# An expert stage in which the 16 prompt rows lie as 128 rows of 128 columns

## What is computed

```python
cap = CAPACITY_FACTOR * T // N_EXPERTS          # 16 prompt rows, 256 sample rows
aff = softmax(h @ w_router)
gates, idx = top_k(aff.T, cap)
xg = h[idx]
y = (silu(xg @ w_gate[e]) * (xg @ w_up[e])) @ w_down[e]
y = y * gates
out = zeros.at[idx].add(y)                      # x = x + gate2 * out, then the final RMSNorm
```

## Time and profile before

| | |
|---|---|
| median of 3 runs | 3281.63 us (3280.39 to 3283.32) |
| the profiled execution | 3282.97 us |
| its span in the trace | 3281.2 us |
| PE busy in the span | 3083.0 us (94%) |
| expert stage | about 1961 us to the end |

### The profile page before, as it was taken

One profiled execution on the slowest core, in us unless ns is written; L12 is line 12 of the kernel. 1 busy time (PEld: TensorE's weight loads), 2 busy tenths in 40 slices (PEclk: granted clock), 3 DMA queues, 4 the chain that ended last, 5 costly groups with the idle time before them and its releaser, 6 DMA issues. The chain is left out here.

```text
span 3281.2 us, 58620 instructions
## 1 busy us (share of the span) xinstructions
PE 3083.0 (94%) x21488; PEld 2804.2 (85%) x21488; DVE 1850.1 (56%) x3184; ACT 1710.9 (52%) x3368; POOL 422.2 (13%) x396
## 2 busy tenths in 40 slices
PE   8999997899999999999899749999999999999996
PEld 4788886688888888888788649999999999999995
DVE  3222225788888888888533485445455455455455
ACT  3222224577777777777433345454454454544454
POOL 0333335500000000000000010111111111111103
PEclk9999998899999999999899759999999999999998
DMA  6222116400000000000164305566665666666656
GB/s 238 70 74 73 65 57 201 163 17 23 23 19 29 19 22 22 21 27 28 63 205 153 116 31 190 182 190 184 184 190 181 190 186 185 187 189 185 190 171 264
DMA packets 318188, 394.61 MB, mean 120 GB/s; under 512 B 30132, under 2 KB 274312, under 8 KB 317080
## 3 DMA queue, kind: packets, MB, share of 16 engines
q1 hardware_dynamic: 307160, 356.11, 32.8%
q0 software_dynamic: 10560, 36.77, 5.0%
q10 hardware_dynamic: 384, 0.62, 0.1%
HBM read 319.54 MB, written 74.06 MB: 120 GB/s over the span
## 5 line engine op out<-in xcount | busy, mean ns | idle before, releaser
L2654 DVE TENSOR_TENSOR e_w_lo<-e_raw,e_w_hi 128x2048 fp32r<-128x2048 f32 x192 | 440.0, 2292 | 476.2 <-ACT e_w_hi L2584 468.8
L92 PE MATMUL e_ps<-e_x_hi,e_w_hi 128*128 128x272 f32 x2048 | 602.2, 294 | 3.4 <-issue 3.4
L94 PE MATMUL e_ps<-e_x_hi,e_w_lo 128*128 128x272 f32 x2048 | 593.9, 290 | 0.0
L93 PE MATMUL e_ps<-e_x_lo,e_w_hi 128*128 128x272 f32 x2048 | 590.1, 288 | 0.0
L1613 DVE TENSOR_TENSOR a_pT_lo<-a_ps_t,a_pT_hi 128x512 fp32r<-128x512 f32 (+1 forms) x648 | 368.0, 600 | 139.5 <-ACT a_pT_hi L1522 139.1
L1522 ACT ACTIVATE a_pT_hi<-a_ps_t 128x512 fp32r<-128x512 f32 (+1 forms) x648 | 319.4, 532 | 172.4 <-PE a_ps_t L1391 165.3
L92 PEld LDWEIGHTS e_ps<-e_x_hi,e_w_hi 128*128 128x128 f32 x2048 | 386.3, 189 | 5.0 <-issue 3.5
L93 PEld LDWEIGHTS e_ps<-e_x_lo,e_w_hi 128*128 128x128 f32 x2048 | 387.0, 189 | 0.0
L94 PEld LDWEIGHTS e_ps<-e_x_hi,e_w_lo 128*128 128x128 f32 x2048 | 386.0, 188 | 0.0
L2584 ACT ACTIVATE e_w_hi<-e_raw 128x2048 fp32r<-128x2048 f32 x189 | 360.4, 1907 | 0.0
L1586 DVE TENSOR_REDUCE a_mx<-a_ps_s 128x1 f32<-128x896 f32 (+2 forms) x392 | 345.9, 890 | 22.8 <-PE a_ps_s L1381 22.8
(11 more groups left out here) (318 smaller groups left out, 5355.8 us busy)
## 6 DMA issues: line engine op xcount, KB each, us to landing
e_raw<-in_w_gate SPq DMA_DIRECT2D x64, 1024.0 KB, 5.0
e_raw<-in_w_up SPq DMA_DIRECT2D x64, 1024.0 KB, 5.0
e_raw<-in_w_down SPq DMA_DIRECT2D x64, 1024.0 KB, 5.0
s_ret<-p_pr SPq DMA_DIRECT2D x17, 768.0 KB, 3.6
p_raw<-in_w_in SPq DMA_DIRECT2D x8, 1152.0 KB, 18.7
o_cT<-s_ct SPq DMA_DIRECT2D x17, 512.0 KB, 5.0
s_x<-o_x SPq DMA_DIRECT2D x17, 512.0 KB, 5.0
s_xn<-o_xn SPq DMA_DIRECT2D x17, 512.0 KB, 3.4
```

Of the source, the lines that this page charges most:

```text
L92: nc.tensor.matmul(out, w_hi, x_hi, start=first, stop=False)
L93: nc.tensor.matmul(out, w_hi, x_lo, start=False, stop=False)
L94: return nc.tensor.matmul(out, w_lo, x_hi, start=False, stop=last)
L2654: nc.vector.tensor_tensor(w_lo[n % RING][:, :, :], raw[n % RING][:, :, :], w_hi[n % RING][:, :, :].bitcast(F32), ALU.subtract).then_inc(w_ ...
```

## The change

The 16 prompt rows of 1024 columns are handled as 128 rows of 128 columns: partition c * 16 + t holds block c of row t.

- Lists. `hot_c` becomes 128 x 128: it compares slot with `again_b`, which counts 0 to 15 eight times. So each of the 128 partitions gets the number of its row; `token[:, e, 2]` is eight times the row plus `which`, the number of the block. ACT's two copies per expert in `keep` become one. A 0/1 matrix `alike` marks the partitions that belong to one row.
- Rows in. The third gather reads 128 pieces of 512 B into `e_xg_c`. One transpose turns all of it (j = 0); the sample rows are turned four pieces in a row, two blocks at a time (j = 1 to 4): 17 transposes in place of 24, in bursts of 5, 4, 4 and 4 after chunks 3, 4, 5 and 7. DVE gives the prompt part scale and shift in two instructions for all blocks (`context`, in n = 4); ACT keeps the 256-column ones. PE's j = 2 waits for `xc_scaled`, the first of DVE's two.
- Sums out. `e_yT_c` and `e_yg_c` are apart. q = 0 is one transpose for the prompt rows, q = 1 to 4 four each: 17 in place of 24, in bursts of 5, 8 and 4 after chunks 0, 1 and 2. POOL adds the prompt pieces first.
- The end. The sum of squares of a prompt row lies in 8 partitions and is put together by one matmul with `alike`. The weight vector is loaded again as `f_w_c` by eight small transfers on SP. The prompt list goes first through the last norms and scatters.

The core of the diff:

```diff
@@ selection, ACT and DVE
             def keep(e):
                 act.wait_ge(hot_mm, e + 1)
-                nc.scalar.activation(got[:, e, 0:2, :].rearrange("p b v -> p (b v)"), ps_got[e % 2][:, 0:2 * NVAL], ACT.Copy)\
+                nc.scalar.activation(got[:, e, :, :].rearrange("p b v -> p (b v)"), ps_got[e % 2][:, 0:3 * NVAL], ACT.Copy)\
                     .then_inc(got_ok, 1)
-                nc.scalar.activation(got[0:CAP_CTX, e, 2, :], ps_got[e % 2][0:CAP_CTX, AT_C:AT_C + NVAL], ACT.Copy).then_inc(got_ok, 1)
...
+                if r == 1:
+                    nc.vector.tensor_scalar(g["weights"].alike[:, :], dist[:, :], 0.0, None, ALU.is_equal)
+                    nc.vector.tensor_scalar(which[:, :], row16[:, :], 1.0 / CAP_CTX, None, ALU.mult)
...
-                nc.vector.tensor_scalar(hot_c[j][:, :], iota_b[:, 0:CAP_CTX], slot[:, NT, e:e + 1], None, ALU.is_equal)
+                nc.vector.tensor_scalar(hot_c[j][:, :], again_b[:, :], slot[:, NT, e:e + 1], None, ALU.is_equal)
...
-            link(nc.vector.tensor_copy(g["token"][:, :, :].rearrange("p e h -> p h e"), rest[:, 0:3, :]))
+            nc.vector.tensor_copy(g["token"][:, :, 0:2].rearrange("p e h -> p h e"), rest[:, 0:2, :])
+            link(nc.vector.tensor_scalar(g["token"][:, :, 2], rest[:, 2, :], float(DC), which[:, 0:1], ALU.mult, ALU.add))
@@ FirstWeights
-    def gather(self, pool, xn_rows, token):
-        for n, m in enumerate([P, P, CAP_CTX]):
-            pool.indirect_dma_start(self.xg[0:m, n, :], None, xn_rows,
-                                    bass.IndirectOffsetOnAxis(ap=token[0:m, 0, n:n + 1], axis=0)).then_inc(self.xg_in, 16)
+    def fetch(self, pool, rows, token, e):
+
+        for n in range(2):
+            pool.indirect_dma_start(self.xg[:, n, :], None, rows.rearrange("t p d -> (t p) d"),
+                                    bass.IndirectOffsetOnAxis(ap=token[:, e, n:n + 1], axis=0)).then_inc(self.xg_in, 16)
+        pool.indirect_dma_start(self.xg_c[:, :], None, rows.rearrange("t p (c d) -> (t p c) d", d=P),
+                                bass.IndirectOffsetOnAxis(ap=token[:, e, 2:3], axis=0)).then_inc(self.xg_in, 16)
@@ experts
-        SUMS_AFTER = {0: (0, 1), 1: (2, 3), 2: (4, 5)}
-        ROWS_AFTER = {3: (0, 1), 4: (2, 3), 5: (4, 5), 7: (6, 7)}
+        SUMS_AFTER = {0: (0, 1), 1: (2, 3), 2: (4,)}
+        ROWS_AFTER = {3: (0, 1), 4: (2,), 5: (3,), 7: (4,)}
@@ SP
             sp.dma_start(wf[:, :], a["norm_f_w"].rearrange("(o d) -> o d", o=1).broadcast_to([P, D])).then_inc(wf_in, 16)
+            for c in range(DC):
+                sp.dma_start(wf_c[c * CAP_CTX:(c + 1) * CAP_CTX, :],
+                             a["norm_f_w"][c * P:(c + 1) * P].rearrange("(o d) -> o d", o=1).broadcast_to([CAP_CTX, P])).then_inc(wf_in, 16)
@@ PE, turn_rows
-                for n, m in enumerate(ROWS):
-                    ins = nc.tensor.transpose(ps_t[b][:, n * P:n * P + m], xg[0:m, n, c * P:(c + 1) * P],
-                                              g["ident"][0:m, 0:m])
+                elif j == 2:
+                    pe.wait_ge(xc_scaled, e + 1)
...
+                if j == 0:
+                    ins = nc.tensor.transpose(ps_t[b][:, 0:P], xg_c[:, :], g["ident"][:, :])
+                else:
+                    for h in range(2):
+                        for n in range(2):
+                            c = 2 * (j - 1) + h
+                            ins = nc.tensor.transpose(ps_t[b][:, h * CAP + n * P:h * CAP + (n + 1) * P],
+                                                      xg[:, n, c * P:(c + 1) * P], g["ident"][:, :])
                 ins.then_inc(x_turned, 1)
@@ PE, turn_sums
-                for c in range(4):
-                    ins = nc.tensor.transpose(ps_t[q % 2][0:m, c * P:(c + 1) * P], yT[:, half_at * 4 + c, n * P:n * P + m],
-                                              g["ident"][:, :])
+                if q == 0:
+                    ins = nc.tensor.transpose(ps_t[0][:, 0:P], yT_c[:, :, :].rearrange("p c t -> p (c t)"), g["ident"][:, :])
+                else:
+                    n, half_at = (q - 1) // 2, (q - 1) % 2
+                    for c in range(4):
+                        ins = nc.tensor.transpose(ps_t[q % 2][:, c * P:(c + 1) * P], yT[:, half_at * 4 + c, n * P:(n + 1) * P],
+                                                  g["ident"][:, :])
@@ PE, the end
-            for q in range(6):
+            for q in range(SUMS):
                 turn_sums(NE - 1, q)
+                if q == 3:
+                    pe.wait_ge(sq_ok, NTA + 1)
+                    nc.tensor.matmul(ps[0][:, 0:1], early.alike[:, :], ss[:, NTA:NTA + 1], start=True, stop=True).then_inc(ss_c_ok, 1)
@@ ACT, start of expert 0
-            for c in range(0, DC, 2):
-                rows(0, c)
-            act.wait_ge(xT_ok, 2 * DC)
+            rows(0, 1)
+            rows(0, 3)
+            act.wait_ge(xc_ok, 1)
+            act.wait_ge(xT_ok, 2)
+            act.wait_ge(xT_odd, 2)
             nc.scalar.activation(x_hi[:, 0:DC // 2, :], xT[:, 0:DC // 2, :], ACT.Copy).then_inc(x_hi_half, 1)
+            act.wait_ge(xT_ok, DC)
@@ DVE
+            def context(e):
+                dve.wait_ge(x_turned, e * TURNS + 1)
...
+                nc.vector.tensor_tensor(xT[:, :, CAP:SLOTS], ps_t[0][:, 0:P].rearrange("p (c t) -> p c t", c=DC),
+                                        g["gain"][:, 1, :, CTX:CTX + 1].broadcast_to(by_chunk), ALU.mult).then_inc(xc_scaled, 1)
+                dve.wait_ge(xc_scaled, e + 1)
+                nc.vector.tensor_tensor(xT[:, :, CAP:SLOTS], xT[:, :, CAP:SLOTS],
+                                        g["mod"][:, SHIFT2:SHIFT2 + DC, CTX:CTX + 1].broadcast_to(by_chunk), ALU.add).then_inc(xc_ok, 1)
```

More of the change, by code:

```diff
@@ L2011, in selection @@
         iota_i, iota_b = k.sb("s_iota_i", [P, P], I32), k.sb("s_iota_b", [P, P], BF16)
+        again_i, again_b = k.sb("s_again_i", [P, DC, CAP_CTX], I32), k.sb("s_again_b", [P, P], BF16)
+        which = k.sb("s_which", [P, 1])
         row_i = k.sb("s_row_i", [P, 1], I32)
@@ L2017, in selection @@
         hot = [k.sb(f"s_hot{i}", [P, NT, P], BF16) for i in range(2)]
-        hot_c = [k.sb(f"s_hot_c{i}", [P, CAP_CTX], BF16) for i in range(2)]
+        hot_c = [k.sb(f"s_hot_c{i}", [P, P], BF16) for i in range(2)]
         far = k.sb("s_far", [P, ON_ACT, P], BF16)
@@ L2070, in _ @@
             pool.wait_ge(token_ok, 1)
-            g["weights"].gather(pool, s["xn"].rearrange("t p d -> (t p) d"), g["token"])
+            g["weights"].fetch(pool, s["xn"], g["token"], 0)
         @block.tensor
@@ L2347, in experts @@
         AHEAD = 3
-        ROWS = [P, P, CAP_CTX]
-        raw, w_hi, w_lo, xg, weights = early.raw, early.w_hi, early.w_lo, early.xg, early.chunk
+        TURNS, SUMS = 5, 5
+        raw, w_hi, w_lo, xg, xg_c, weights = early.raw, early.w_hi, early.w_lo, early.xg, early.xg_c, early.chunk
         xT = k.sb("e_xT", [P, DC, SLOTS])
@@ L2467, in _ @@
                 scatter(e)
[L2469 removed]
+            pool.wait_ge(x_turned, NE * TURNS)
             pool.wait_ge(y_out, LAST * 48)
[L2471 to L2473 removed]
+            early.fetch(pool, s["x1"], g["token"], LAST)
             pool.wait_ge(half_ok, 1)
@@ L2584, in split, with rows @@
                 nc.scalar.activation(w_hi[n % RING][:, :, :], raw[n % RING][:, :, :], ACT.Copy).then_inc(w_hi_ok, 1)
-            def rows(e, c):
-                if c == 0 and not (isinstance(e, int) and e == 0):
+            def rows(e, j):
+                if j == 1 and not (isinstance(e, int) and e == 0):
                     act.wait_ge(x_lo_ok, e)
-                act.wait_ge(x_turned, e * DC + c + 1)
-                for lo, hi, who in ((0, CAP, LAT), (CAP, SLOTS, CTX)):
-                    nc.scalar.activation(xT[:, c, lo:hi], ps_t[c % 2][:, lo:hi], ACT.Identity,
-                                         bias=g["mod"][:, SHIFT2 + c, who:who + 1],
-                                         scale=g["gain"][:, 1, c, who:who + 1]).then_inc(xT_ok, 1)
+                act.wait_ge(x_turned, e * TURNS + j + 1)
+                for h in range(2):
+                    c = 2 * (j - 1) + h
+                    nc.scalar.activation(xT[:, c, 0:CAP], ps_t[j % 2][:, h * CAP:(h + 1) * CAP], ACT.Identity,
+                                         bias=g["mod"][:, SHIFT2 + c, LAT:LAT + 1],
+                                         scale=g["gain"][:, 1, c, LAT:LAT + 1]).then_inc(xT_ok, 1)
             def rows_hi(e):
-                act.wait_ge(xT_ok, (e + 1) * 2 * DC)
+                act.wait_ge(xT_ok, (e + 1) * DC)
+                act.wait_ge(xc_ok, e + 1)
                 if not (isinstance(e, int) and e == 0):
@@ L2611, in body @@
                     if not last:
-                        for c in ROWS_AFTER.get(n - 1, ()):
-                            rows(e + 1, c)
+                        for j in ROWS_AFTER.get(n - 1, ()):
+                            if j:
+                                rows(e + 1, j)
                         if n == 8:
```

(23 more changed lines are left out.)

173 lines of the change are left out of this document (84 added, 89 removed).

## The result

| us | before | after |
|---|---|---|
| median (4 runs each) | 3281.01 (3280.00 to 3283.32) | 3222.32 (3221.62 to 3224.40) |
| profiled execution | 3282.97, span 3281.2 | 3224.40, span 3222.7 |

The ratio is 0.982, with a 95% interval of 0.9808 to 0.9832: 1.8% faster. The direction and the large term were right, the size was not.

What follows compares the result with a forecast made beforehand. PE was taken to bound the expert loop. Loop -46.8, selection +1.5, start of expert 0 -2.5 and end -1.5 summed to -49.3 us, median 3281.63 to 3232.3, forecast 3232, range 3224 to 3245.

Steps and rivals of the forecast that it cites:

- the large term: Expert loop: fewer, all full transposes on PE save 3.12 us in each of 15 experts, 46.8 us.
- rival 2: PE's transposes: only their count matters, the gap stays in each burst; gain 21 us, 3258; chance 0.05.
- (a): Loop, chunk 4: PE's j = 2 waits for DVE's first prompt instruction, with 0.7 us of slack.
- (b): Loop, chunk 8: PE needs the last `e_h_lo`; with a shorter burst ahead, 0.5 us of slack is left.
- rival 1: Loop: a new wait at (a) or (b) gives back 4.5 to 15 us, 3237 to 3247; chance 0.10.
- The start: Expert 0: fewer turns, half of `e_x_hi` made meanwhile; PE begins at about 1971.8, -2.5 us (0 to -4).
- rival 3: SP's queue blocks on the eight broadcast loads, 15.73 us each: slower, 3346; chance 0.02.
- the end: After the last expert: smaller prompt sums and norms, sample list issued last at about 3269; -1.5 us (+1 to -3).
- the "linear" bound: Loop: a burst's price goes with its length, 34 x 0.109 = 3.71 us an expert, gain 50 us.
- the selection: Routing on DVE: wider one-hot +1.0 us, with other new instructions together +1.5 us.
- the other new instructions: Selection on DVE: `alike` and `which` 0.23 and some 0.15, the split token instruction 0.1 us.
- rival 4: Change does more than said: no price of a burst, start gains 4; 3221; chance 0.08.

Runs made afterwards that it cites:

- b_rows128: Kernel before, prompt list gathered and turned as 128 rows instead of 16, the count of transposes kept: 3255.17 us, ratio 0.9917 to before.
- a_late3: Changed kernel with three unused 128x512 VectorE adds ahead of the prompt instructions in each expert: 3240.63 us.
- a_head_old: Changed kernel, first half of x's high part waiting for all turned rows in expert 0: 11.79 us from stage start to first product, against 10.65.
- a_fw_early: Changed kernel with SP issuing the final norm's weights in expert 0 instead of ahead of the last expert's rows: 3224.91 us.
- b_hotc_wide: Kernel before, VectorE writing the selection's prompt one-hot 128 columns wide while PE reads 16: one-hot loop 2.41 us an expert, as before.
- a_prompt_last: Changed kernel with the prompt list issued last at the end: 1363.1 us from the selection on, against 1362.9.
- b_prompt_first: Kernel before with the last expert's prompt list issued ahead of the two sample lists: 1420.7 us from the selection on, against 1420.2.
- b_sems3: Kernel before with three more, unused semaphores: 8.8 us from last data to end of span, 10.3 from last issue, as before.

## Why the prediction was wrong

**Right, and shown.** PE alone bounds the loop, and every microsecond taken from it counts: period 76.35, PE busy in all of it. The 16-row piece is what costs: b_rows128 gets 1.79 of the 3.33 us by adding rows. The waits on "issue" are gone, and rival 2 (count only) with them. The covers (a) and (b) hold, with 0.7 and 0.3 us that can be used, so rival 1 did not come about; a_late3 shows what it would have cost. The start gave 2.36 of 2.5, by the step named (a_head_old). SP's eight issues cost 0.48 us each, not 15.73, and are hidden (a_fw_early): rival 3 falls.

In the loop, then, the mechanism was right and one price in it was off. At the end 3.3 us came from something that the forecast had no term for.

**Wrong: the price of a full piece.** I split the 0.87 us of a burst of 8 into 8 x 0.099 and 0.08 for the burst. That split rested on one length of burst with full pieces alone, and all the bursts of the earlier trace rows fit it. It is 0.109 a piece and nothing for the burst, the "linear" bound of the text, which stood there at 50 us: 49.8 measured, and the bursts of 4, 5 and 8 leave zero for a burst. The term of 46.8 was 3.0 too small.

**Wrong: the selection.** +1.5 forecast, -0.4 measured. Most of it is the one-hot: I priced the widened one at the pace of its neighbours (0.19) and left the neighbours as they were. It came to 0.16, and the others got faster, which one trace can't tell. A loss was the only sign that I had considered. Off by 1.9, of which b_hotc_wide explains 16 x 0.06 = 1.0. The forecast's 0.5 for the other new instructions was not tested, and the stretch differs by up to 0.6 between traces of kernels that are alike in it.

**Wrong: the end.** -1.5 forecast, bound -3, -4.7 measured. Up to the last issue it is -2.2, in line with the step (the last issue some 2 us sooner); a_prompt_last gives 1.5 of it to the order. I had added that the last sample list would land later after its issue, which it does, by 0.7 to 0.8. But 3.3 us vanished behind the last data. For that stretch I had no term, and no reason for leaving it out; no row showed one, and b_prompt_first, a_prompt_last and b_sems3 did not find one: the cause of the largest part of the miss stays open. Off by 3.2.

**The range.** 3.0 + 1.9 + 3.2, less 0.1 at the start, plus 1.2 us by which this execution reached the selection sooner, is the whole miss of 9.2 between the spans; between the medians it is 9.7. The low end of 3224 took half of rival 4 and let its parts add up only in a case of chance 0.08. But the linear price and the end were independent unknowns with bounds that I had written down; 50 us in the loop and -3 at the end alone give 3227.6, and a selection term of -0.4 gives 3225.7. With the few microseconds by which runs of one kernel differ, the low end belonged at 3220; that is said with the result known.

## What to carry to other kernels

Ahead of counting instructions on a bound engine, look for odd shapes among them: a stationary of 16 rows among ones of 128 cost three full ones here, and padding it to 128 rows, with more data moved, made the kernel 0.8% faster by itself. When one burst length is all a trace shows, the split into a price per piece and a price per burst is not determined; carry both splits to the range. And the traces reached the same point in the middle, behind the same code, up to 7.7 us apart, while 3.3 us behind the last data went with the program for a reason not found: compare stretches between marks, not spans.
